# A gated convolution layer on one core: two gaps in SBUF shift TensorE's operands by 384 and 768 bytes

## The chip, the core and the metric

The kernel runs on one core of one Trainium2 chip. The metric is the device time of one execution in microseconds (us). SBUF is the on-chip memory of 128 partitions from which TensorE (PE in the profile) reads both operands of a matmul; PSUM takes the results. VectorE is DVE, ScalarE is ACT, GpSimd is POOL, SyncE is SP. All addresses below are bytes within one partition, and "mod 512" is the rest of an address after division by 512.

## What is computed

One layer of the trunk, with 1,024 tokens and 1,024 channels (depth 1, so only the convolution mixer runs). Cut to what matters:

```python
def conv_mixer(h, w_in, conv_w, conv_b, ln_g, ln_b, w_out):
    z = h @ w_in                                   # 1024 x 3072
    a, b, gate = jnp.split(z, 3, axis=-1)
    u = a * jax.nn.sigmoid(b)
    u = causal_depthwise_conv(u, conv_w) + conv_b  # 31 taps
    uf = layer_norm(u) * ln_g + ln_b
    u = jax.nn.silu(uf) * jax.nn.silu(gate)
    return u @ w_out
# result: x + conv_mixer(rms_norm(x, norm_g), ...)
```

All of it is float32. The kernel keeps that precision with a split: every matrix is written as a high part that TensorE's one-pass format (fp32r) holds and a low part that is the rest, and each product is three matmuls, high by high, high by low and low by high.

## The kernel before

**Tiling.** Tokens come in two halves of 512, channels in eight blocks of 128. A unit is one block of 128 output columns of `w_in`; there are 24, and `UNITS` gives their order (b and a of each block, then the gates). A unit needs, for each half, 8 blocks of input channels with 3 terms each: 24 matmuls with a stationary operand of 128x128 and a moving operand of 128x512.

**TensorE's order** is written out by hand. After `WARM_UPS` small matmuls on `ones` (L738), `project_raw` (L610) does the first two units while their inputs arrive, `project` and `unit_terms` (L593) do the other 22 units. In these the stationary operand is a block of `w_hi` or `w_lo` and the moving one a half row of `x_hi` or `x_lo`. Between them stand `spread_rms` (L583 and L588, twice each: stationary `ones_r`, moving `diags`), the transposes of the convolved channels (L665: `nat` and `ident`) and `spread_mean` and `spread_rstd` (L673, L683). Last comes `out_product` (L692), seven products of the output projection (the two halves on both sides are combined so that seven do for eight). There the roles are the other way round: the stationary operand is a 128x128 block of `x_hi` or `x_lo`, which by now hold the gated values, and the moving one a row of `wb_hi` or `wb_lo`. In all TensorE runs 1,480 matmuls of 512 columns, 24 of 256 and 128 short ones.

**The others.** ACT rounds to the high parts, applies sigmoid and SiLU and makes tap products; DVE and POOL make the low parts (L1051, L1059, L1400) and add up the taps of the convolution (L1131, L1456). SP issues nearly all DMAs: in the first 18 us the transposed input into `nat` (L473), rows of the input into `sgate` (L469), for their sums of squares, and the first weights into `raw` (L485, L478). Later one unit's weights (512 KB) arrive about every 11 us.

**Where the buffers lie.** `sb(name, shape, dtype)` takes the next free address in each partition; a buffer's address follows from the sizes of those ahead of it. The first one starts at 1,152, behind 1,024 bytes of descriptor space and four constants. Buffers opened in the `first` stack are freed before those of the output projection are opened, so `wb_hi` and `wb_lo` take their place. The listing shows the function with the allocations.

Of the kernel before, what the change touches and what calls it, by code (L numbers as in the profile page):

```python
# [10 lines left out]
P = 128  # L11
# [90 lines left out]
def gated_conv_layer(nc, x, x_t, w_in, w_out, per_channel, identity, out):  # L102
# [31 lines left out]
    with ctx:  # L134
        def sb(name, shape, dt=F32, into=ctx):
            return into.enter_context(nc.sbuf_tensor(name, shape, dt))

        def sem(name):
            return ctx.enter_context(nc.semaphore(name))

        nat = sb("nat", [P, NT, D])
        x_hi = sb("x_hi", [P, KC, T], F32R)
        x_lo = sb("x_lo", [P, KC, T], F32R)
# [15 lines left out]
        w_even = chan[:, 4 * KC:KC * (4 + HT)].rearrange("p (j k) -> p j k", k=HT)  # L159
        w_odd = chan[:, KC * (4 + HT):KC * (4 + 2 * HT)].rearrange("p (j k) -> p j k", k=HT)  # L160

        sig = sb("sig", [P, 2, HALF])


# [1386 lines left out]
```

## Time and profile before

| | us |
|---|---|
| median of 3 runs | 369.41 (369.32 to 369.87) |
| the profiled execution | 369.1 |
| its span, first to last instruction | 367.3 |
| PE busy | 363.2 (99% of the span) |
| DVE busy | 321.2 (87%) |
| POOL busy | 263.1 (72%) |
| ACT busy | 209.1 (57%) |
| TensorE's granted clock, mean | 0.999 of 2.4 GHz |

The profiled execution's time is 1.8 us more than its span, and 0.3 us less than the median. Busy time of PE is the time in which at least one matmul is in flight; matmuls overlap, so that a matmul of 512 columns is recorded with some 395 ns while the next one starts some 233 ns after it. The distance from start to start is therefore the number to read. A chain of work, as the profile gives it, follows the last instruction back to what released it; for a run of matmuls that wait for nothing its length divided by their count is that distance.

### The profile page before, as it was taken

To read this page: it belongs to the slowest core of one execution; us is meant where nothing else is said; L and a number is where in the kernel's file an instruction comes from. 1 tells how busy PE (TensorE), PEld (TensorE's weight loads), DVE (VectorE), ACT (ScalarE), POOL (GpSimd) and SP (SyncE) were. 2 spreads that over 40 slices of the span, in tenths; PEclk is the share of its full clock that TensorE was granted. 3 is DMA by queue.
4 is the path that set the end of the run, shared out by engine and by line. 5 is a ranking of instruction groups with operands and counts; after the bars stand their busy time and mean duration, and the time that the engine had idled before them with its cause. 6 is when DMAs were issued, how large, how long until landed. Compare 5 with 4: busy or idle time off the path is not lost.

```text
span 367.3 us, 4866 instructions
## 1 busy us (share of the span) xinstructions
PE 363.2 (99%) x1622; PEld 295.7 (81%) x1622; DVE 321.2 (87%) x514; ACT 209.1 (57%) x321; POOL 263.1 (72%) x198
## 2 busy tenths in 40 slices
PE   8999999999999999999999999999999999999997
PEld 7878788888888888888888888888888888888886
DVE  5678799999999899998999999963789989997952
ACT  6889785568446633874666757643436880442400
POOL 0119999999999996999999999996676431313230
PEclk9999999999999999999999999999999999999999
DMA  7995011301111011111011110113213785047142
GB/s 252 403 401 208 20 57 57 111 6 57 57 59 58 1 59 57 57 59 49 9 60 57 57 57 3 57 59 138 90 59 115 257 326 218 0 115 260 52 167 98
DMA packets 13849, 39.33 MB, mean 107 GB/s; under 512 B 1664, under 2 KB 2176, under 8 KB 13824
## 3 DMA queue, kind: packets, MB, share of 16 engines
q1 hardware_dynamic: 13680, 39.01, 29.4%
q8 instruction: 13, 0.21, 0.2%
q14 instruction: 12, 0.10, 0.1%
q10 hardware_dynamic: 144, 0.00, 0.0%
HBM read 34.82 MB, written 4.19 MB: 106 GB/s over the span
## 4 chain that ended last, share of the span: by engine, by line
PE 93%; SPq 2%; DMA 2%; DVE 1%; issue 1%; ACT 0%
PE mm L593 67%; PE acc L692 12%; PE mm L692 9%; DMA sgate<-x 2%; PE mm L665 2%; PE mm L610 2%; SPq L473 1%; PE acc L683 0%; PE acc L673 0%; SPq L485 0%; ACT sgate L756 0%; SPq L469 0%; DVE diags L1033 0%; DVE x_lo L1051 0%; SPq L491 0%
## 5 line engine op out<-in xcount | busy, mean ns | idle before, releaser
L593 PE MATMUL mm<-x_hi,w_hi 128*128 128x512 f32 x352 | 139.9, 397 | 0.0
L593 PE MATMUL mm<-x_hi,w_lo 128*128 128x512 f32 x352 | 139.1, 395 | 0.0
L593 PE MATMUL mm<-x_lo,w_hi 128*128 128x512 f32 x352 | 139.0, 395 | 0.0
L1131 DVE SCALAR_TENSOR_TENSOR acc<-u,chan,acc 128x512 f32<-128x512 f32 x154 | 108.5, 751 | 0.1
L593 PEld LDWEIGHTS mm<-x_hi,w_lo 128*128 128x128 f32 x352 | 66.3, 188 | 15.4
L1456 POOL TENSOR_TENSOR pconv<-pconv,prod 128x512 f32<-128x512 f32 x60 | 78.6, 1353 | 0.0
L593 PEld LDWEIGHTS mm<-x_lo,w_hi 128*128 128x128 f32 x352 | 66.4, 189 | 15.1
L593 PEld LDWEIGHTS mm<-x_hi,w_hi 128*128 128x128 f32 x352 | 66.3, 188 | 15.1
L1131 DVE SCALAR_TENSOR_TENSOR acc<-u,w_sum,acc 128x512 f32<-128x512 f32 x90 | 67.6, 751 | 0.2
L853 ACT ACTIVATE prod<-u,chan 128x512 f32<-128x512 f32 x73 | 50.7, 718 | 18.4 <-POOL pconv L1456 15.2
L1456 POOL TENSOR_TENSOR pool_before<-pool_before,prod 128x512 f32<-128x512 f32 x41 | 54.6, 1331 | 1.6
L1400 POOL TENSOR_TENSOR w_lo<-raw,w_hi 128x1024 fp32r<-128x1024 f32 (+1 forms) x21 | 50.3, 2394 | 3.3 <-ACT w_hi L803 3.2
L692 PE MATMUL acc<-wb_hi,x_lo 128*128 128x512 f32 (+1 forms) x68 | 26.0, 382 | 0.0
L692 PE MATMUL acc<-wb_hi,x_hi 128*128 128x512 f32 (+1 forms) x68 | 26.0, 382 | 0.0
L692 PE MATMUL acc<-wb_lo,x_hi 128*128 128x512 f32 (+1 forms) x68 | 26.0, 382 | 0.0
L803 ACT ACTIVATE w_hi<-raw 128x1024 fp32r<-128x1024 f32 x22 | 23.2, 1054 | 3.9 <-PE mm L593 2.6
L853 ACT ACTIVATE prod<-u,w_sum 128x512 f32<-128x512 f32 x30 | 21.5, 718 | 5.5 <-POOL pool_before L1456 5.0
L820 ACT ACTIVATE sgate<-mm 128x512 f32<-128x512 f32 x16 | 9.6, 597 | 26.4 <-PE mm L593 26.3
L905 ACT ACTIVATE x_hi<-sgate 128x512 fp32r<-128x512 f32 x28 | 15.6, 622 | 11.2 <-DVE sgate L1207 11.2
L1219 DVE TENSOR_TENSOR nat<-acc,nat 128x512 f32<-128x512 f32 (+1 forms) x22 | 13.7, 661 | 7.9 <-PE acc L692 7.9
L1389 POOL TENSOR_TENSOR x_lo<-nat,x_hi 128x512 fp32r<-128x512 f32 x16 | 20.3, 1294 | 0.2 <-ACT x_hi L796 0.2
L692 PE MATMUL mm<-wb_lo,x_hi 128*128 128x512 f32 x48 | 19.0, 395 | 0.0
(112 smaller groups left out, 518.4 us busy)
## 6 DMA issues: line engine op xcount, KB each, us to landing
raw<-w_in SPq DMA_DIRECT2D x22, 512.0 KB, 3.2
nat<-x_t SPq DMA_DIRECT2D x16, 256.0 KB, 6.1
sgate<-x SPq DMA_DIRECT2D x8, 512.0 KB, 10.7
raw<-w_out SPq DMA_DIRECT2D x8, 512.0 KB, 3.2
nat<-x SPq DMA_DIRECT2D x8, 512.0 KB, 5.4
y<-nat SPq DMA_DIRECT2D x15, 256.0 KB, 2.3
raw_late<-w_out SPq DMA_DIRECT2D x4, 512.0 KB, 4.0
sig<-w_out SPq DMA_DIRECT2D x4, 512.0 KB, 5.1
```

What stands on the lines that cost most here:

```text
L593: ins = nc.tensor.matmul(bank(("unit", m, h)), w[:, m % 3, k, :], xx[:, k, half(h)], start=(k == 0 and i == 0), stop=(k == KC - 1 and i == 2))
L610: return nc.tensor.matmul(bank(("unit", m, h)), w[:, m, k, :], xx[:, k, half(h)], start=(k == 0 and i == 0), stop=(k == KC - 1 and i == 2))
L692: ins = nc.tensor.matmul(product_bank(b, q), v[:, k0 + k, rows], w[:, k, piece_columns(b, q)], start=(k == 0 and i == 0 and continued(b, q ...
L803: nc.scalar.activation(w_hi[:, m % 3, :, :].rearrange("p k n -> p (k n)"), raw[:, m % 2, :], ACT.Copy).then_inc(whi_ready, 1)
L820: nc.scalar.activation(sgate[:, j, h * HALF:(h + 1) * HALF], bank(("unit", m, h)), ACT.Silu).then_inc(g_read, 1)
L853: nc.scalar.activation(dst, chain_in(j, chain, k), ACT.Identity, scale=tap(j, chain, k), bias=bias(j, chain) if k == 0 else 0.0).then_inc( ...
L905: nc.scalar.activation(v_pair(b, k)[0], v_raw(b, k), ACT.Copy).then_inc(vhi_ready, 1)
L1131: ins = nc.vector.scalar_tensor_tensor(dst, chain_in(j, chain, k), tap(j, chain, k), chain_bank(j, chain), ALU.mult, ALU.add)
L1219: nc.vector.tensor_tensor(total, product_bank(b, q), total, ALU.add).then_inc(post_done, 1)
L1389: nc.gpsimd.tensor_tensor(x_lo[:, k, half(h)], nat[:, k, half(h)], x_hi[:, k, half(h)].bitcast(F32), ALU.subtract).then_inc(xlo_pool, 1)
L1400: nc.gpsimd.tensor_tensor(w_lo[:, m % 3, ks, :].rearrange("p k n -> p (k n)"), raw[:, m % 2, ks.start * P:], w_hi[:, m % 3, ks, :].rearran ...
L1456: ins = nc.gpsimd.tensor_tensor(pool_sum(chain), summand, prod[:, SLOTTED.index((j, chain, k)) % 4, :], ALU.add)
```

## The change

Two buffers that nothing reads or writes, of 96 float32 (384 bytes) per partition, are allocated: one ahead of `nat`, one ahead of `sig`. No instruction is added, removed or moved on any engine.

```diff
@@ -138,6 +138,7 @@
         def sem(name):
             return ctx.enter_context(nc.semaphore(name))
 
+        sb("lead_gap", [P, 96])
         nat = sb("nat", [P, NT, D])
         x_hi = sb("x_hi", [P, KC, T], F32R)
         x_lo = sb("x_lo", [P, KC, T], F32R)
@@ -159,6 +160,7 @@
         w_even = chan[:, 4 * KC:KC * (4 + HT)].rearrange("p (j k) -> p j k", k=HT)
         w_odd = chan[:, KC * (4 + HT):KC * (4 + 2 * HT)].rearrange("p (j k) -> p j k", k=HT)
 
+        sb("middle_gap", [P, 96])
         sig = sb("sig", [P, 2, HALF])
```

Addresses in the two programs as built, which follow from the sizes:

```
buffer                     before    mod 512    after     mod 512
nat                          1152      128        1536        0
x_hi                        33920      128       34304        0
x_lo                        66688      128       67072        0
sgate                       99456      128       99840        0
raw                        132224      128      132608        0
chan                       140416      128      140800        0
ident                      141568      256      141952      128
ones                       142080      256      142464      128
sig                        144128      256      144896        0
w_hi, wb_hi3               148224      256      148992        0
w_lo                       160512      256      161280        0
spare                      164608      256      165376        0
u, wb_hi0                  172800      256      173568        0
other wb_hi, wb_lo            ...      256         ...        0
prod, rows                    ...      480         ...      224
pconv                      218624        0      219392      256
raw_late                   221952      256      222720        0
ones_r                     222720        0      223488      256
diags                      223232        0      224000      256
```

A 128-column block of a weight is 512 bytes and a half row of `x_hi` 2,048 bytes, so all blocks of one buffer have the same rest. What lies ahead of `middle_gap` moves by 384 bytes, what lies behind it by 768; both are multiples of 128, so no address changes its rest modulo 128. The rest of x_hi, x_lo and w_hi, w_lo modulo 512 becomes 0 in all of the large products, as stationary and as moving operand. Five small operands of TensorE go the other way: `ident` and `ones` from 256 to 128, and `ones_r` and `diags` from 0 to 256; `mean_var` and `rstd` stay off any such multiple.

## Rows read from the trace of the kernel before

**Rows 1.** The page: busy us (share of the span), instructions.

```profile
PE 363.2 (99%) x1622; PEld 295.7 (81%) x1622; DVE 321.2 (87%) x514; ACT 209.1 (57%) x321; POOL 263.1 (72%) x198
```

**Rows 2.** The chain that ended last, whole span: start us, us, what, count.

```profile
37.69 45.50 PE mm L593 x195
84.06 36.25 PE mm L593 x156
161.98 33.46 PE mm L593 x144
270.80 15.34 PE mm L593 x66
286.13 5.60 PE acc L692 x24
...
297.33 11.20 PE acc L692 x48
...
336.53 11.20 PE mm L692 x48
```

**Rows 3.** Timeline of PE, 361.3 to 362.6: start us, us, instruction.

```profile
361.57 0.28 PE L692 MATMUL acc<-wb_hi,x_hi 128*128 128x256 f32 x1
...
362.52 0.28 PE L692 MATMUL acc<-wb_hi,x_lo 128*128 128x256 f32 x1
```

**Rows 4.** Timeline of PE, 24.0 to 26.2, around the first spread of the scales.

```profile
24.39 0.39 PE L610 MATMUL mm<-x_hi,w_lo 128*128 128x512 f32 x1
24.62 0.40 PE L583 MATMUL acc<-diags,ones_r 128*128 128x512 f32 x1
24.86 0.39 PE L588 MATMUL acc<-diags,ones_r 128*128 128x512 f32 x1
25.09 0.40 PE L610 MATMUL mm<-x_hi,w_hi 128*128 128x512 f32 x1
25.32 0.39 PE L610 MATMUL mm<-x_lo,w_hi 128*128 128x512 f32 x1
```

**Rows 5.** Timeline of PE, 284.8 to 287.6, where the output projection begins.

```profile
285.26 0.40 PE L593 MATMUL mm<-x_hi,w_hi 128*128 128x512 f32 x1
285.50 0.40 PE L593 MATMUL mm<-x_lo,w_hi 128*128 128x512 f32 x1
...
285.97 0.40 PE L692 MATMUL acc<-wb_hi,x_hi 128*128 128x512 f32 x1
286.20 0.39 PE L692 MATMUL acc<-wb_lo,x_hi 128*128 128x512 f32 x1
286.43 0.40 PE L692 MATMUL acc<-wb_hi,x_lo 128*128 128x512 f32 x1
286.67 0.39 PE L692 MATMUL acc<-wb_hi,x_hi 128*128 128x512 f32 x1
```

**Rows 6.** Timeline of PE, 22.0 to 23.9, and what ended its idle time.

```profile
22.67 0.40 PE L610 MATMUL mm<-x_hi,w_hi 128*128 128x512 f32 x1
23.37 0.50 PE L610 MATMUL mm<-x_lo,w_hi 128*128 128x512 f32 x1 [0.30 <-DVE x_lo L1051]
23.70 0.39 PE L610 MATMUL mm<-x_hi,w_lo 128*128 128x512 f32 x1
```

**Rows 7.** The chain that ended last, 0 to 26 us: start us, us, what.

```profile
10.14 8.18 DMA sgate<-x
18.32 0.02 issue
18.34 1.15 ACT sgate L756 x2
```

**Rows 8.** DMA issues of the page: queue, count, KB each, median us to landing.

```profile
raw<-w_out SPq DMA_DIRECT2D x8, 512.0 KB, 3.2
...
raw_late<-w_out SPq DMA_DIRECT2D x4, 512.0 KB, 4.0
```

## The prediction, made before the changed kernel was run

> **What bounds the kernel now.** First the busy times of the page: PE is busy for 363.2 of 367.3 us [rows 1], and no other engine comes near. So the question is not who waits for whom but how far apart TensorE starts its matmuls. For that I read the chain that ended last, in order of time, which is nearly all PE, in long runs that wait for nothing. A run's length divided by its count is the distance from start to start: 45.50 us over 195 matmuls is 233.3 ns, 36.25 over 156 is 232.4, 33.46 over 144 is 232.4, 15.34 over 66 is 232.4, and in the output projection 11.20 over 48 is 233.3 [rows 2]. Two distances, then, 0.9 ns apart. The short one holds for most of L593, the long one for the run that begins at 37.69 and for all of L692. By the counts of these runs some 520 of the 1,480 wide matmuls go at 233.3 and some 960 at 232.4, a mean of 232.7. The profiled execution's own sum is 1,480 x 232.7 ns = 344.4 us of wide matmuls and 22.9 us of everything else in the span (the start until inputs are there, 24 matmuls of 256 columns, the short ones, the last add and store), plus 1.8 us around the span: 369.1. The median of the runs is 0.3 us above this, at 369.4. I forecast for that median.
>
> **What the change could reach.** It has one part: addresses move by 384 or 768 bytes. No instruction is touched, so apart from a different speed of the very same accesses there is nothing to gain or lose. Since PE has no slack behind it, every nanosecond per wide matmul is 1.48 us, 0.4% of the time.
>
> First, how a wide matmul's 232.4 ns are made up. From the first to the ninth start of 256 columns it is 0.95 us, 118.8 ns each [rows 3]. From 256 to 512 columns the distance grows by 113.6 ns, 0.444 ns per column, and what is left over per matmul is 232.4 - 512 x 0.444 = 5.2 ns. The granted clock of 0.999 of 2.4 GHz would be 0.417 ns per column. So there are two amounts which alignment might in principle touch: 5.2 ns fixed per matmul, and 512 x 0.027 = 14 ns that grows with columns.
>
> An address that is off a boundary touches one more chunk of memory per operand than one that is on it, whatever the number of columns. If that costs anything it sits in the fixed part. The part that grows with columns crosses the same number of boundaries per kilobyte wherever it begins; alignment should not touch it. This bounds a plausible gain at 5.2 ns x 1,480 = 7.7 us, and a less plausible one at (232.7 - 213.3) x 1,480 = 28.7 us.
>
> Does the trace show operands at either rest? Three kinds of matmul are in it. L593 has its moving operand at 128 and its stationary one at 256 (mod 512). L692 has them the other way round, 256 and 128. And the four of L583 and L588 have both, `ones_r` and `diags`, at 0, exactly what the change gives to all the others. **This is the row the forecast rests on**: the first pair starts at 24.62 and 24.86, the next matmul at 25.09 and the one behind it at 25.32 [rows 4]. That is 0.24, 0.23 and 0.23 us, with 0.23 ahead of them: 234 ns for a fully aligned matmul followed by a fully aligned one, to the 10 ns that the row shows, and no sign of 229 or 213. L593 alone has both 232.4 and 233.3 with the same addresses [rows 2], so the 0.9 ns are not a matter of the rest alone either. The bound from both sides is thus: nothing (rows 4), and the fixed 5.2 ns in either direction. I take nothing, since rows 4 are the only ones with the new rests. They are four matmuls, read to 10 ns, so they exclude 213 well and 229 only weakly.
>
> **The rule that speaks for more.** Rows 2 and 3 have 232.4 ns at 512 columns. The Trainium skill (TensorE: Matmul & The Clock Gate, section "Wait — 56ns, not 53.3ns?") gives N/2.4 GHz plus about 2.5 ns, 215.7 ns measured at 512 columns of bf16. The trace disagrees with it by 17 ns, and if misalignment were why, the sum by that page would be some 344 us; it does not say that a 4-byte operand keeps this rate, which is as good an explanation.
>
> **Other engines and DMAs.** DVE, ACT and POOL read and write at other addresses as well, but no rest modulo 128 changes and all three hide behind PE. What they do at the start does not hide: PE waits at 22.67 (0.70 us to the next start, and 0.33 to the one after, 0.57 more than twice 232) [rows 6], and the chain there goes back to an 8.18 us transfer of rows into `sgate` [rows 7]. Its destination goes from 128 to 0 modulo 256. If that makes it faster, at most these 0.57 us come back, as nothing else in the stretch is long. The rows nearest to it speak against that: 512 KB into `raw` (rest 128) land in 3.2 us and into `raw_late` (rest 0 modulo 256) in 4.0 [rows 8]. I count zero. The Trainium skill (DMA: Bandwidth & Descriptors, section "How a descriptor splits into AXI transactions") says that a descriptor which starts off a 256-byte boundary costs an extra partial transaction; it speaks for this small gain, and rows 8 do not bear it out.
>
> **The rivals.**
>
> *The pattern of distances shifts (chance 0.21).* At 285.97 L692 begins, without any wait, and the starts, until then one 0.24 among several 0.23, at once alternate between 0.23 and 0.24 [rows 5], the long distance. A change of operands alone did that. So addresses can choose between the two patterns, and new ones may choose anew. If all go at 232.4 the sum is 520 x 0.9 ns = 0.5 us lower, 368.9; if all go at 233.3 it is 960 x 0.9 = 0.9 us higher, 370.3. The same can come from a start that is a little earlier or later: the run at 233.3 begins at 37.69, right behind the second pair of L583 and L588, and the next one, at 84.06 behind eight short matmuls, is back at 232.4 [rows 2]. I give 0.04 to faster than 368.7 (with the start's 0.57 us), 0.09 to no difference, 0.08 to 370.2 and above.
>
> *The fixed part shrinks (0.17).* One fewer chunk per operand takes 1 to 5 of the 5.2 ns away: 1,480 x 3 ns = 4.4 us at the middle, 365.0; 361.7 at the end. For it speaks that rows 4 can't exclude it and that a fixed part is there at all; against it that swapping the rests 128 and 256 between the operands (L692 against L593) leaves the fixed part within 1 ns.
>
> *The column part shrinks (0.03).* All matmuls at the granted clock: 28.7 us off, 340.7. Rows 4 are against it, three distances of which each would be 20 ns shorter.
>
> *The two operands collide: slower (0.08).* Before, the moving operand and the stationary block that is loaded beside it started 128 bytes apart modulo 512; after, both start at 0 in every product. If the memory serves both from the same place at the same time, each matmul goes at what is now the longest member of the pattern, 0.24 us [rows 5]: (240 - 232.7) x 1,480 = 10.8 us, 380.2. It decides as soon as it costs 0.5 ns per matmul, as nothing hides it. Against it are rows 4 again, both at 0 and not at 0.24 twice. The Trainium skill (SBUF — State Buffer, section "Who interferes with whom") gives PE two independent read ports, which speaks against this too; that two operands never meet in one memory bank it does not say.
>
> *Only the start moves (0.03).* 0.57 us at most: 368.8, not told from no change.
>
> **How the numbers follow.** No effect has the rest, 0.48: 369.4, within the spread of the runs. A measurement of this kernel tells 0.2%, some 0.7 us, from no change. Faster by more: 0.04 + 0.17 + 0.03 = 0.24. Slower by more: 0.08 + 0.08 = 0.16. Within: 0.48 + 0.09 + 0.03 = 0.60. The range reaches to the long pattern everywhere, 370.5 with the runs' spread, and down to the middle of the fixed part's case, 365.0. Outside stay the lower half of that case (0.08), the column part (0.03) and the collision (0.08), 0.19 together. The likeliest case by itself is 369.1 to 369.9.
>
> **What would show it right or wrong.** Right: in the chain of the changed kernel the long runs of L593 and L692 divide to 232.4 and 233.3 ns, in whatever shares, and the 256-column matmuls to 119 ns. The pattern rival: the same two values, but L692 or the run from 37 us with the other one. The fixed part: 512 and 256 columns shorter by the same nanoseconds, and L583 and L588, which lose their alignment, not. The column part: 512 columns shorter by twice what 256 are. The collision: both stages above 234. The start: the distance behind 22.67 falls to 0.23 while all others stay. What would prove me wrong is that four matmuls at 10 ns are too few to speak for 1,480.

## The result: 6.5 us faster, and every wide matmul 6 ns closer to the last

| | before | after |
|---|---|---|
| median, us | 369.37 (369.24 to 369.87, 4 runs) | 362.90 (362.62 to 363.05, 4 runs) |
| ratio | | 0.9826, 95% interval 0.9814 to 0.9838 |
| span of the profiled execution, us | 367.3 | 360.8 |
| PE busy, us | 363.2 | 354.3 |

The forecast was no change, 369.4 us with a range from 365.0. The time fell below the range.

The chain of the changed kernel that ended last, in order of time (start us, us, what, count), answers to [rows 2]; the lines of the code are two or less further down than before (L593 is L595, L692 is L694):

```profile
143.06 16.36 PE mm L595 x72
160.28 32.66 PE mm L595 x144
193.82 27.22 PE mm L595 x120
...
266.79 15.00 PE mm L595 x66
281.79 5.44 PE acc L694 x24
...
292.67 10.88 PE acc L694 x48
...
330.75 10.88 PE mm L694 x48
```

32.66 us over 144 matmuls is 226.8 ns, 15.00 over 66 is 227.3 (the first few matmuls behind a break are slower, and they weigh more in a short run) and 10.88 over 48 is 226.7. There is one distance instead of two, in both stages: it was 232.4 and 233.3 in [rows 2]. Written out from the trace to the nanosecond the starts are 227, 227, 226 and again, a mean of 226.67 ns, which at the granted clock of 1.00 of 2.4 GHz is 544 cycles for 512 columns.

The matmuls of 256 columns did not get shorter. Timeline of TensorE in the changed kernel (start us, us, instruction):

```profile
356.74 0.28 PE L694 MATMUL acc<-wb_hi,x_lo 128*128 128x256 f32 x1
...
357.46 0.28 PE L694 MATMUL acc<-wb_hi,x_lo 128*128 128x256 f32 x1
```

These are six distances in 0.72 us, 120.0 ns each, where [rows 3] had 118.8.

**Where the rest of the gain went.** For some 960 matmuls the distance is 5.7 ns shorter, for some 520 it is 6.6 ns shorter: 5.5 + 3.4 = 8.9 us. The span fell by 6.5. In the chain of the changed kernel the stretch up to 142 us is no longer PE but mostly POOL, with ACT and a transfer at its start, and the view of PE's waits and its timeline show one place where the two meet:

```profile
PE mm L667 <- POOL nat L1449: 1.9, 1, 1.9
```

```profile
139.71 0.39 PE L595 MATMUL mm<-x_hi,w_lo 128*128 128x512 f32 x1
141.99 1.06 PE L667 MATMUL mm<-ident,nat 128*128 128x128 f32 x8 [1.89 <-POOL nat L1449]
142.81 0.48 PE L595 MATMUL mm<-x_hi,w_hi 128*128 128x512 f32 x1
```

The start at 139.71 is followed by the next one 2.28 us later instead of 0.23: TensorE arrives at the transposes of channel block 1 before POOL has summed that block up. This wait did not exist before; it gives back 2.05 us. The rest of the difference is small: 0.15 us more of waiting ahead of the spread at 36 us, and 0.25 us of transients (the mean distance in L595 is 226.9, not 226.7, since the first few matmuls behind each break are longer). 8.9 - 2.05 - 0.15 - 0.25 is 6.45. At the start nothing changed in sum: the waits for inputs ahead of the first spread at 24 us lie elsewhere (a new one of 0.7 us for ACT near 6 us, none behind 22.7), but they add up to 1.1 us in both traces. Of the 1,622 matmuls in either trace 1,480 have 512 columns, 24 have 256, and 118 (not 128) are short.

### The profile page after: what moved, and what is told of

It reads as the page before. It is cut to its first block, busy times and chain, and to the rows that moved or that the text cites. A ratio compares the mean times of both kernels' runs of the same rounds, so it can differ in the third digit from the quotient of the medians.

```text
span 360.8 us, 4866 instructions
## 1 busy us (share of the span) xinstructions
PE 354.3 (98%) x1622; PEld 294.6 (82%) x1622; DVE 321.3 (89%) x514; ACT 209.0 (58%) x321; POOL 262.7 (73%) x198
## 4 chain that ended last, share of the span: by engine, by line
PE 60%; POOL 17%; issue 14%; DMA 3%; SPq 3%; ACT 3%; DVE 1%; ACTq 0%
PE mm L595 36%; PE acc L694 12%; PE mm L694 9%; POOL x_lo L1391 5%; POOL pconv L1458 4%; POOL w_lo L1402 3%; DMA raw<-w_in 3%; SPq L475 2%; POOL u L1436 2%; PE mm L667 2%; POOL pool_before L1458 1%; ACT prod L855 1%; ACT w_hi L805 1%; ACT diags L780 1%; PE acc L685 0%
## 5 line engine op out<-in xcount | busy, mean ns | idle before, releaser
L595 PE MATMUL mm<-x_hi,w_hi 128*128 128x512 f32 x352 | 138.0, 392 | 0.0
L595 PE MATMUL mm<-x_hi,w_lo 128*128 128x512 f32 x352 | 137.0, 389 | 0.0
L595 PE MATMUL mm<-x_lo,w_hi 128*128 128x512 f32 x352 | 137.0, 389 | 0.0
L595 PEld LDWEIGHTS mm<-x_hi,w_lo 128*128 128x128 f32 x352 | 66.1, 188 | 13.8
L595 PEld LDWEIGHTS mm<-x_hi,w_hi 128*128 128x128 f32 x352 | 66.1, 188 | 13.4
L595 PEld LDWEIGHTS mm<-x_lo,w_hi 128*128 128x128 f32 x352 | 66.1, 188 | 13.3
L694 PE MATMUL acc<-wb_lo,x_hi 128*128 128x512 f32 (+1 forms) x68 | 25.6, 377 | 0.0
L694 PE MATMUL acc<-wb_hi,x_lo 128*128 128x512 f32 (+1 forms) x68 | 25.6, 376 | 0.0
L694 PE MATMUL acc<-wb_hi,x_hi 128*128 128x512 f32 (+1 forms) x68 | 25.6, 376 | 0.0
L694 PE MATMUL mm<-wb_hi,x_hi 128*128 128x512 f32 x48 | 18.7, 389 | 0.0
L694 PE MATMUL mm<-wb_lo,x_hi 128*128 128x512 f32 x48 | 18.7, 389 | 0.0
```

The lines of the kernel that those rows point to most:

```text
L595: ins = nc.tensor.matmul(bank(("unit", m, h)), w[:, m % 3, k, :], xx[:, k, half(h)], start=(k == 0 and i == 0), stop=(k == KC - 1 and i == 2))
L694: ins = nc.tensor.matmul(product_bank(b, q), v[:, k0 + k, rows], w[:, k, piece_columns(b, q)], start=(k == 0 and i == 0 and continued(b, q ...
```

## Experiments: whose start counts

First, one operand at a time. Each of the four kernels differs from the changed one only in the sizes of the two gaps; "x" stands for `x_hi` and `x_lo`, "w" for `w_hi`, `w_lo`, `wb_hi` and `wb_lo`, the numbers are their starts modulo 512.

**x at 0, w at 256.**

```diff
-        sb("middle_gap", [P, 96])
+        sb("middle_gap", [P, 32])
```

> Gaps of 384 and 128 bytes: x_hi and x_lo start at 0 modulo 512, w and wb at 256 as in the kernel before. Theory M (only the moving operand's start counts): L593's matmuls, with x moving, go at 226.7 ns as with both at 0, L692's, with wb moving, stay at 233.3; time 369.4 - 1,156 x 5.8 ns + what is lost to a new wait (up to 2 us) = 363 to 365 us. Theory S (only the stationary operand counts): the other way round, L692 at 226.7, L593 at 232.4; 369.4 - 324 x 6.6 ns = 367.2 us. Theory E (each operand off a multiple of 512 costs by itself, or both must be on one): both stages between 226.7 and 233.3, or both unchanged at 369.4. Theory R (the two operands must have the same rest): both unchanged, 369.4.

**x at 128, w at 0.**

```diff
-        sb("lead_gap", [P, 96])
-        sb("middle_gap", [P, 96])
+        sb("middle_gap", [P, 64])
```

> One gap of 256 bytes ahead of sig: x at 128 as before, w and wb at 0. The mirror image of the first run. Theory M: L593 stays at 232.4, L692 (wb moving) at 226.7, 367.2 us. Theory S: L593 at 226.7, L692 at 233.3, 363 to 365 us. Theory E: both in between or both unchanged. Theory R: unchanged, 369.4 us.

**x at 128, w at 128.**

```diff
-        sb("lead_gap", [P, 96])
```

> Only the gap of 384 bytes ahead of sig: x and w both at 128 modulo 512. Theory R (same rest, whatever it is): 226.7 ns in both stages, 362.9 us. Theories M, S and E (a multiple of 512, or of 256): no gain, 232 to 234 ns in both stages, 369.4 us; worse than before if a rest of 128 costs more than one of 256.

**x at 256, w at 256.**

```diff
-        sb("lead_gap", [P, 96])
+        sb("lead_gap", [P, 32])
```

> Gaps of 128 and 384 bytes: x and w both at 256 modulo 512. If a multiple of 256 is enough, 226.7 ns in both stages and 362.9 us; then rest 128 was the only fault of the kernel before. If it must be 512, 232 to 234 ns and 369.4 us. Theory R: 362.9 us as well, so that this run tells M, S and E from R only together with the one before.

Measured, with the distances as the chain gives them for 144 matmuls of the first stage and 48 of the output projection:

| kernel | median, us | ratio to before | first stage, ns | output projection, ns |
|---|---|---|---|---|
| x 0, w 256 | 362.93 | 0.9819 (0.9805 to 0.9834) | 226.8 | 226.7 |
| x 128, w 0 | 369.48 | 0.9999 (0.9990 to 1.0009) | 232.4 | 233.3 |
| x 128, w 128 | 363.54 | 0.9848 (0.9824 to 0.9872) | 226.8 | 226.7 |
| x 256, w 256 | 363.18 | 0.9834 (0.9811 to 0.9858) | 226.8 | 226.7 |

The rows behind the first two, from the chain of x 0, w 256 and then of x 128, w 0:

```profile
160.24 32.66 PE mm L595 x144
266.75 15.00 PE mm L595 x66
292.62 10.88 PE acc L694 x48
```

```profile
162.30 33.46 PE mm L594 x144
271.12 15.34 PE mm L594 x66
297.65 11.20 PE acc L693 x48
```

Moving and stationary operand swap places between the stages, and yet the stages always go together. That rules out theories M and S: with x at 0 and w at 256, whichever of the two is moving, it is fast. Theory E falls too, since x and w both at 128 is fast, no multiple of 256 or 512 being in sight. Theory R, that the rests modulo 512 must be equal, is nearly right, but 0 and 256 are not equal, and it had expected no gain from x at 0, w at 256. What fits all six kernels so far is: **the starts of the two operands must differ by a multiple of 256 bytes**. Before, they differed by 128. I call it R256 below.

R256 was formed after these runs, so it had to forecast something. Two kernels for that, with one gap each.

**x at 128, w at 384.** No operand on a multiple of 256, but the difference is 256. It is also the smallest edit of all, 128 bytes.

```diff
-        sb("lead_gap", [P, 96])
-        sb("middle_gap", [P, 96])
+        sb("middle_gap", [P, 32])
```

> One gap of 128 bytes ahead of sig and none in front: x stays at 128 modulo 512, w and wb go to 384. No operand of the large products is then on a multiple of 512 or of 256, but both have the same rest modulo 256. The theory formed from the first runs (R256: what counts is that the two operands' starts differ by a multiple of 256 bytes) expects 226.7 ns in both stages and 362.9 to 363.5 us. Theories of alignment of an operand by itself expect 232 to 234 ns and 369.4 us.

**x at 0, w at 128.** The front gap of the change alone, with nothing in the middle.

```diff
-        sb("middle_gap", [P, 96])
```

> Only the gap ahead of nat: x at 0, w and wb at 128. One of the two operands is on a multiple of 512, the difference is 128. R256 expects no gain, 232.3 to 233.4 ns and 369.4 us. A theory that the gap ahead of nat was what helped (x0_w256 was fast, x128_w0 was not) expects 226.7 ns and 362.9 us.

The single gap of 128 bytes took 363.57 us, ratio 0.9839 (0.9825 to 0.9852); the front gap alone 369.55 us, ratio 1.0002 (0.9991 to 1.0013). The chains, of x 128, w 384 first, then of x 0, w 128:

```profile
161.04 32.66 PE mm L594 x144
293.43 10.88 PE acc L693 x48
```

```profile
162.22 33.46 PE mm L594 x144
297.57 11.20 PE acc L693 x48
```

Both came out as R256 said and against any alignment of an operand by itself. So the change does not help because the operands are on multiples of 512. It helps because the difference between their starts went from 128 to 0 modulo 256.

## Experiments: the cost by itself

**A map.** Behind the last product and the last add of the changed kernel, 26 blocks of 48 matmuls on buffers that are full by then, each block with its own pair of starts and width. The block for 128 and 0, as an example (one float32 is 4 bytes):

```diff
+            pe.wait_ge(post_done, len(POSTS))
+            for n in range(48):  # moving 128 mod 512, stationary 0, 512 columns
+                nc.tensor.matmul(acc[:, 2, 0:512], wb[0][0][:, n % CK, 0:0+P], x_hi[:, n % KC, 32:32+512], start=True, stop=True)
```

> The changed kernel with 26 blocks of 48 matmuls added behind its last product and the last add; their results are not used. Each block has one pair of starts modulo 512 (bytes) of the moving and of the stationary operand, and one width. Theory of lines (one extra cycle per 64 bytes of the moving operand, nothing else if aligned): 544 cycles, 226.7 ns, at 512 columns with both at 0, 170 ns at 384; a start of the moving operand off its boundary adds 4 to 7 ns, whatever the width. If 64-byte lines are what counts, starts of 128 and 256 go as 0 and only 4 to 32 bytes cost; if 512, all of them cost. Columns theory (a part that grows with the width): an offset costs half at 256 of what it costs at 512. At 256 columns, both kernels show 119 to 120 ns, which may be the stationary load and then hides an offset.

**A second map** with 27 blocks more, in the same way. Three of them mix starts; the one that copies the situation of [rows 4] is:

```diff
+            for n in range(72):  # moving 128, but twice 0 in every 24, stationary 0
+                nc.tensor.matmul(acc[:, 2, 0:512], wb[0][0][:, n % CK, 0:P], x_hi[:, n % KC, (0 if n % 24 in (10, 11) else 32):(0 if n % 24 in (10, 11) else 32) + 512], start=True, stop=True)
```

> The changed kernel with 27 blocks of matmuls behind its last product, results not used. R256: equal small rests (4 and 4, 32 and 32, 64 and 64 bytes) all go at 226.7 ns at 512 columns; differences of 64 and 192 do not. Blocks where two matmuls of difference 0 stand in a stream of difference 128, as the pairs of L583 and L588 stood in the kernel before: if it takes several matmuls until the short distance is reached (the first map: 4 to 6), these two go at 231 to 236 ns, which shows why the rows that I rested on could not tell. If not, they go at 227 and those rows must have another reason. Widths: an aligned matmul takes N cycles of 2.4 GHz plus 32, so 133.3 ns at 288, 160 at 352, 186.7 at 416, 213.3 at 480 columns; with a difference of 128 the added time grows from below zero at 256 columns to 6.7 ns at 512.

The chain of the first map has one row per block. Here are moving 128, 256 and 384 with stationary 0 (L754, L756, L758), stationary 128 and 256 with moving 0 (L768, L770), both at 128 (L776), both at 256 (L778), and 384 columns without and with a difference of 128 (L790, L792):

```profile
371.39 11.19 PE acc L754 x48
382.58 10.89 PE acc L756 x48
393.48 11.19 PE acc L758 x48
...
449.34 11.15 PE acc L768 x48
460.49 10.88 PE acc L770 x48
...
493.72 10.91 PE acc L776 x48
504.63 10.88 PE acc L778 x48
...
555.05 8.32 PE acc L790 x48
563.37 8.45 PE acc L792 x48
```

Divided by 48 that is 233.1, 226.9, 233.1, 232.3, 226.7, 227.3, 226.7, 173.3 and 176.0 ns. Free of the first matmuls of a block, the distances of both maps are these (mean of the last 30 to 40 starts of a block, from the trace; "difference" is moving minus stationary start modulo 256; the granted clock was 1.00 in all these stretches):

```
512 columns   difference   0 (0/0, 256/0, 0/256, 32/32, 64/64, 128/128, 256/256)   226.7 ns
512 columns   difference  64 (64/0, 0/192)                                         228.9
512 columns   difference 128 (128/0, 384/0, 128/256, 256/128)                      233.3
512 columns   difference 128 (0/128)                                               232.3
512 columns   difference 192 (192/0, 0/64, 64/128, 256/64)                         233.3
512 columns   32/0   233.3     16/0   231.6     0/4   232.5     4/0   236.7     4/4   237.8
columns               128    192    256    288    320    352    384    416    448    480    512
difference 0        111.7  111.7  120.0  131.7  146.7  161.1  173.3  188.3  202.7  216.7  226.7
difference 128      111.7  111.7  118.7  133.3  146.7  158.3  176.0  190.0  204.0  217.8  233.3
```

Three things follow. One, R256 holds with the operands isolated, for starts on multiples of 32 bytes. A moving operand 4 bytes off costs 10 to 11 ns, even if the stationary one is off alike, and a stationary one off by itself 5.8; the expectation that 4 and 4 would go at 226.7 failed. Two, the cost is in no way a constant per matmul: it is 6.7 ns at 512 columns, 2.7 at 384, nothing at 320, below zero at 256 and at 352. That contradicts both the theory that an offset adds 4 to 7 ns whatever the width and the one that it costs half at 256 of what it costs at 512; nor does it simply grow from 256 to 512, as I expected of the second map. Three, at 256, 320, 384 and 512 columns with difference 0 the distance is the columns at 2.4 GHz plus 13.3 ns; at other widths it is not so regular. The first map's theory of lines, which asks for 170 ns at 384 columns, failed (173.3), and so did the second map's expectation of N + 32 cycles at 288, 352, 416 and 480, by 1 to 3 ns and with either sign.

The last block of the second map (128/0 with the same stationary and the same moving block every time) went at 233.3 ns as well, so the cost does not come from going to another block.

The mixed block shows why the rows that I rested on could not tell. Distances in ns out of the trace, from the eighth start of the block on; the two matmuls with both operands at 0 are in brackets:

```
map2, 128/0 with two of 0/0:  238, 229, 237, [230, 236], 234, 229, 238, 229
before, L583 and L588:        232, 228, 230, [234, 231], 235, 228, 238, 229
```

A pair with difference 0 inside a stream of difference 128 is no faster than its surroundings. The changed kernel has the counterpart. There `diags` and `ones_r` are both at 256, so that their difference is 0 as it was before, but now all their neighbours have it too, and the same pair starts 0.23 us apart, 227 and 226 ns out of the trace:

```profile
24.05 0.39 PE L585 MATMUL acc<-diags,ones_r 128*128 128x512 f32 x1
24.28 0.39 PE L590 MATMUL acc<-diags,ones_r 128*128 128x512 f32 x1
```

In a block of its own a difference of 0 takes 1 to 7 matmuls until 226.7 is reached (226, 233, 230, 227 at 32/32; 230, 224, 231, 236, 228, 232, 231, 227 at 64/64). Where twelve matmuls of 0/0 and twelve of 128/0 take turns, each twelve reaches its own distance; where single ones take turns, the mean is 230.0. The maps say how fast a steady stream is, and so do the kernels; for a matmul taken alone there is no such number.

The mixed block also explains the two distances of the kernel before. It starts with 229 and 238 in turn, 233.3 on average. Behind its second pair the same 128/0 matmuls go in a pattern of seven (232, 232, 228, 230, 233, 241, 232), 232.4 on average, and behind the third pair they are back at 229 and 238. So at one and the same difference of 128 what went before selects one of two patterns, and the 232.3 of 0/128 in the table is the second of them rather than a matter of these starts: with the front gap alone, the first two units (x moving at 0, w at 128) went at 233.3.

## Experiments: what was given back, and the start

**The wait for POOL.** One line of the order table of the changed kernel: the transposes of channel block 1 half a unit later.

```diff
-                   (11, 1): [(1, 0), (1, 1)],
+                   (12, 0): [(1, 0), (1, 1)],
```

> The changed kernel with one line of the order table edited: the transposes of channel block 1, which POOL sums up, come half a unit later on TensorE and ACT. Theory G (the 2.05 us at 139.7 us, where TensorE waits for POOL, is a part of the gain given back, and no other wait takes its place): that wait goes, 362.9 - 2.0 = 360.9 us. Rival: POOL, whose work is fixed, makes TensorE wait at a later block or in the norm instead, and the time stays within 0.5 us of 362.9.

360.69 us (360.55 to 361.80), ratio to before 0.9777 (0.9762 to 0.9793), 2.2 us faster than the changed kernel. The view of PE's waits holds no POOL any more, and the chain is PE again; its row for the run that took 45.50 us in [rows 2] is the last line here:

```profile
PE acc L740 <- DVE ones L1022: 1.0, 1, 1.0
PE mm L612 <- ACT x_hi L764: 0.2, 1, 0.2
```

```profile
37.01 44.20 PE mm L595 x195
```

The given-back part is thus shown, and no kernel here has a lower median.

**The same with the single gap.** The edit of x 128, w 384 and that of the later transposes together.

> The single gap of 128 bytes with the later transposes of channel block 1. By R256 and by the run with the later transposes: 360.7 us, as with both gaps. If the front gap gives something at the start by its transfers into nat, sgate and raw (up to 0.6 us), 361.3 us.

361.30 us (360.86 to 362.11), ratio 0.9780 (0.9764 to 0.9797). The intervals of the two kernels overlap; they are not told apart.

**The changed kernel again**, on the chip of the single gap.

> The changed kernel once more, on the same chip as the single gap: 362.9 us. Its distance to the single gap is the worth of the rest of the buffers (transfers, other engines): zero if only the pair of operands counts, up to 0.6 us if the transfers at the start count too.

362.65 us, ratio 0.9826 (0.9805 to 0.9847), against 363.57 for the single gap. At equal distances between matmuls the front gap seems worth 0.6 to 0.9 us. Its candidate is the transfers at the start: `nat`, `sgate` and `raw` go from rest 128 to rest 0 modulo 256. Two kernels separate these buffers from TensorE's operands.

**Transfers at 0, x and w at 128 modulo 256.**

```diff
+        sb("x_gap", [P, 32])
         x_hi = sb("x_hi", [P, KC, T], F32R)
         x_lo = sb("x_lo", [P, KC, T], F32R)
+        sb("sgate_gap", [P, 32])
         sgate = sb("sgate", [P, KC, T])
...
-        sb("middle_gap", [P, 96])
```

> The gap of 384 bytes ahead of nat and one of 128 bytes each ahead of x_hi and of sgate; none ahead of sig. The buffers that the transfers at the start fill (nat, sgate, raw) have rest 0 modulo 256, TensorE's operands x and w both 128. Theory D (the 0.6 to 0.9 us between the kernels with and without the front gap are transfers that land sooner on a multiple of 256 bytes): as with both gaps, 362.7 to 362.9 us. Theory P (TensorE itself, or ACT and DVE on x and w, are slower at the start when x and w have rest 128): 363.5 us, as with the single gap.

**Transfers at 128, x and w at 0 modulo 256.** The same without `lead_gap`.

> The mirror image: gaps of 128 bytes ahead of x_hi and of sgate only. nat, sgate and raw have rest 128 modulo 256, x and w rest 0. Theory D: 363.5 us and waits of TensorE near 22.5 to 26 us, as with the single gap. Theory P: 362.7 to 362.9 us.

363.13 us (362.86 to 363.40), ratio 0.9832 (0.9818 to 0.9845), and 363.53 (363.38 to 365.12), ratio 0.9858 (0.9837 to 0.9878). The direction is theory D's, the difference 0.4 us where it expected 0.6 to 0.9, and the intervals overlap. Theory D's other sign, waits of TensorE near 22.5 to 26 us, doesn't settle it: they are 0.29 us behind 22.97 with transfers at 128 and 0.11 with transfers at 0, but the kernel with the later transposes, whose transfers go to 0, waited 0.29 there too. The windows view of 8 to 22 us, in which the input arrives, tells more (columns: stretch, length, granted clock, share of the DMA engines, GB/s), for transfers at 0 and then for transfers at 128:

```profile
8.00:22.00 14.00, 1.00 1.05 409
```

```profile
8.00:22.00 14.00, 1.00 1.05 400
```

The same view gives 410 for the changed kernel and for front gap alone, 400 for x 128, w 384 and 391 for the kernel before. Over all runs, the kernels whose transfers go to multiples of 256 have 409 or 410, the others 391 to 401, whatever TensorE's operands do. That the transfers run 2 to 3% faster there is shown (5% against the kernel before, the lowest of the others). What it is worth in time, some 0.5 us, is not shown: the medians of the fast kernels point to it, their intervals overlap, and in the front-gap-only kernel the time did not move by anything that can be told.

## Why the prediction was wrong, step by step

- **What bounds the kernel**: right. Every nanosecond per wide matmul is 1.48 us, and PE had no slack. The gain came through the distance between starts. It was not asked how much faster PE could get before another engine bounds it (last point below).
- **The row the forecast rests on**: this step failed. "I take nothing, since rows 4 are the only ones with the new rests." The term put at nothing, the change of distance per wide matmul, measured 5.7 and 6.6 ns, 8.9 us in all. The four matmuls of L583 and L588 do have both operands on 0, and the first pair went at 234 and 231 ns. But the mixed block of the second map reproduces that (230 and 236 for its pair) although a steady stream of such matmuls goes at 226.7. The distance belongs to the stream, with 1 to 7 matmuls of transition, not to the pair. I had written that four matmuls exclude 229 only weakly, and named as what would prove me wrong that they are too few; the chance of no effect, 0.48, did not follow from that.
- **The make-up of the 232.4 ns**: failed. "5.2 ns fixed per matmul, and 512 x 0.027 = 14 ns that grows with columns" drew a line through 256 and 512 columns. The map has no such line: with difference 128 the distance at 256 columns is 118.7 and at 512 it is 233.3, with difference 0 it is 120.0 and 226.7. The first pair makes the cost look proportional, the second shows columns at the full clock plus 13.3 ns. So the bound of 5.2 ns for the gain was no bound (it was 5.7 and 6.6), and the 14 ns that I took for a share of the columns are a fixed part that stays.
- **The rests of L593 and L692 against each other**: read wrongly. Swapping 128 and 256 between the operands left the distance, and I took it as evidence against an effect of addresses. Under R256 a swap can't change anything, since the difference stays 128.
- **The rival "the fixed part shrinks"** (0.17; 365.0 at its middle, 361.7 at its end): nearest in time, and right that addresses alone would do it; its mechanism, a further chunk per operand off a boundary, was wrong, so that 362.9 lies between its two times by luck. Both operands at 128 are as fast as both at 0. Its test, that 512 and 256 columns become shorter by the same, failed as well.
- **The rival "the pattern shifts"** (0.21): the observation was right that addresses choose the pattern. It lacked the thought that there could be a third pattern, one that none of the rows before showed in a long run. Its other thought, that the run from 37.69 is slower because of the pair of L583 and L588 ahead of it, fits the mixed block, where such pairs switched the stream between 233.3 and 232.4.
- **The rival "the operands collide"** (0.08): the right kind of cause, the relation between the two operands, with the wrong sign. I let equal rests be the bad case; a difference of 128 is. What the Trainium skill (SBUF — State Buffer, section "Who interferes with whom") says of two independent read ports of PE does not describe what these runs show: moving one operand's start relative to the other's changes the pace of both stages, from 232.4 and 233.3 ns to 226.7.
- **The rule of 215.7 ns** (the Trainium skill, TensorE: Matmul & The Clock Gate, section "Wait — 56ns, not 53.3ns?"): the form, columns at the clock plus a constant, holds with difference 0 at 256, 320, 384 and 512 columns, but the constant of this kernel's 4-byte operands is 13.3 ns by the map, not 2.5. Some 344 us would have been right if misalignment were why this kernel is 17 ns above that rule; 5.7 to 6.6 of them went with the addresses, 11 stayed.
- **The start**: counted as zero, at most 0.57 us. The landing times of [rows 8] compared transfers at different times under different load and could not show 2%. The rate over 8 to 22 us does, 391 before and 410 after. The rival's sign came true, 0.23 us to the start behind 22.69 in the changed kernel, but a wait of 0.7 us near 6 us was new, and the sum of the waits ahead of the first spread stayed (one trace of each kernel). What the Trainium skill (DMA: Bandwidth & Descriptors, section "How a descriptor splits into AXI transactions") says of starts off 256 bytes is the direction that was measured; it tells of bytes fetched, and gives no rate, while here the destinations moved.
- **What is late next**: not asked. The rivals on the fast side left it out that POOL, 72% busy, hands blocks to TensorE; 2.05 us of 8.9 were given back there.

## What to carry to other kernels

When a stream of matmuls is bound by the distance between its starts, compare that distance with the columns at the granted clock, and look at the two operands' start addresses together: here 512 columns of a 4-byte type started 6 ns closer together as soon as the starts differed by a multiple of 256 bytes, and one gap of 128 bytes was enough. A few matmuls of another kind inside a stream are no sample of how a stream of them would go. And after a faster bound, look at once for the place where the next engine is late; moving one consumer half a unit later was worth another 2.2 us.

## What the runs showed of the hardware that I had not expected

- Moving and stationary reads are not independent of each other's addresses. With starts on multiples of 32 bytes the distance at 512 columns is 226.7 ns at a difference of 0 modulo 256, 228.9 at 64, and 232.3 to 233.3 at 128 and 192. No run shows by what mechanism. The cost changes with the width, its sign too (6.7 ns at 512 columns, -2.7 at 352), and a stream needs 1 to 7 matmuls to settle. At a difference of 128 the same starts go at 232.4 or at 233.3, by what went before.
- Both starts 4 bytes off cost 11 ns at 512 columns, the moving one alone 10, the stationary one alone 5.8.
- Below 256 columns the distance stays at 111.7 ns for these 4-byte operands (128 and 192 columns), with a difference of 0 and of 128.
- Transfers into SBUF ran at 409 to 410 GB/s over 14 us when their destinations started on multiples of 256 bytes, and at 391 to 401 when they were 128 off.
